# Cross attention: order of panel and x splits, banks given back one by one, and the last head's scaling and splits moved

## The reference, cut to what matters

```
h = h + y @ w_out                                  # y: the two attentions' output
h = h + cross_attention(rms_norm(h, g_cross), rms_norm(mem, g_mem), w_xq, w_xkv, w_xo)

q  = x @ w_xq;  k, v = split(memn @ w_xkv)         # 4 heads of 256
s  = q @ k.T / sqrt(256)                           # per head, 1024 x 256
o  = softmax(s) @ v
return o.reshape(1024, 1024) @ w_xo
```

## Time and profile before

| | us |
|---|---|
| median of 3 runs | 2339.19 |
| lowest and highest | 2332.63, 2339.25 |
| profiled execution, its own time | 2333.39 |
| its span | 2331.6 |
| TensorE busy | 2231.5 |
| VectorE busy | 1375.6 |
| ScalarE busy | 950.6 |
| GpSimd busy | 701.7 |

### The profile page before, as it was taken

One profiled execution on the slowest core, in us unless ns is written; L12 is line 12 of the kernel. 1 busy time (PEld: TensorE's weight loads), 2 busy tenths in 40 slices (PEclk: granted clock), 3 DMA queues, 4 the chain that ended last, 5 costly groups with the idle time before them and its releaser, 6 DMA issues.

```text
span 2331.6 us, 36430 instructions
## 1 busy us (share of the span) xinstructions
PE 2231.5 (96%) x14780; PEld 1758.6 (75%) x14780; DVE 1375.6 (59%) x1787; ACT 950.6 (41%) x1680; POOL 701.7 (30%) x436
## 2 busy tenths in 40 slices
PE   7999999998999998999999999999999999999997
PEld 4777766666688887778888888888676677778885
DVE  6767846668576445475664675523508376567654
ACT  4444457777534222253344334223415412264321
POOL 2312211221211222345655464422131133222221
PEclk9999999999999999999999999999999999999999
DMA  3211101113132100111111111112120011100022
GB/s 132 75 52 55 43 21 55 55 46 118 46 115 76 37 28 28 46 38 61 64 36 54 54 51 41 61 46 91 64 83 28 14 42 37 39 19 13 4 109 81
DMA packets 38555, 125.80 MB, mean 54 GB/s; under 512 B 3856, under 2 KB 4368, under 8 KB 37776
## 3 DMA queue, kind: packets, MB, share of 16 engines
q1 hardware_dynamic: 33936, 103.30, 13.1%
q10 hardware_dynamic: 4480, 20.49, 2.3%
HBM read 114.34 MB, written 8.91 MB: 53 GB/s over the span
## 4 chain that ended last, share of the span: by engine, by line
PE 83%; DVE 9%; ACT 5%; issue 2%; DMA 0%; ACTq 0%; DVEq 0%
PE PS L184 22%; PE PS L186 21%; PE PS L185 21%; PE PS L2243 2%; PE PS L744 2%; PE PS L767 1%; PE PS L1192 1%; DVE arena L1013 1%; PE PS L929 1%; PE PS L894 1%; PE PS L911 1%; PE PS L312 1%; PE PS L1853 1%; DVE arena L393 1%; PE PS L1713 1%
## 5 line engine op out<-in xcount | busy, mean ns | idle before, releaser
L184 PE MATMUL PS<-u_r,w_hi 128*128 128x512 f32 x1184 | 479.0, 405 | 18.8 <-DVE h L581 4.4
L233 POOL TENSOR_TENSOR w_hi<-w_raw,const 128x1024 fp32r<-128x1024 f32 x77 | 152.8, 1985 | 1133.2 <-PE PS L184 1079.3
L186 PE MATMUL PS<-u_r,w_lo 128*128 128x512 f32 x1184 | 462.8, 391 | 0.0
L194 POOL TENSOR_TENSOR w_lo<-w_raw,w_hi 128x1024 fp32r<-128x1024 f32 (+1 forms) x143 | 331.6, 2319 | 325.4 <-ACT w_hi L190 310.6
L185 PE MATMUL PS<-arena_r,w_hi 128*128 128x512 f32 (+1 forms) x888 | 331.9, 374 | 0.0
L184 PEld LDWEIGHTS PS<-u_r,w_hi 128*128 128x128 f32 x1184 | 222.9, 188 | 76.1 <-DVE arena_r L194 7.2
L186 PEld LDWEIGHTS PS<-u_r,w_lo 128*128 128x128 f32 x1184 | 222.8, 188 | 47.8
L184 PE MATMUL PS<-h_r,w_hi 128*128 128x512 f32 x512 | 209.4, 409 | 4.3 <-DVE u_r L401 3.9
L186 PE MATMUL PS<-h_r,w_lo 128*128 128x512 f32 x512 | 201.0, 393 | 0.0
L185 PE MATMUL PS<-y_r,w_hi 128*128 128x512 f32 x512 | 199.5, 390 | 0.0
L1508 DVE TENSOR_TENSOR h<-h,PS 128x512 f32<-128x512 f32 x288 | 181.8, 687 | 21.7 <-PE PS L186 17.6
(11 more groups left out here) (431 smaller groups left out, 4292.1 us busy)
## 6 DMA issues: line engine op xcount, KB each, us to landing
w_raw<-in_w SPq DMA_DIRECT2D x174, 512.0 KB, 3.4
arena<-in_w SPq DMA_DIRECT2D x10, 512.0 KB, 5.6
h<-in_xT ACTq DMA_DIRECT2D x1, 4096.0 KB, 14.6
u<-parked_stream ACTq DMA_DIRECT2D x1, 4096.0 KB, 12.8
out<-arena SPq DMA_DIRECT2D x16, 256.0 KB, 2.0
parked_stream<-h ACTq DMA_DIRECT2D x6, 512.0 KB, 2.6
h<-in_xT SPq DMA_DIRECT2D x8, 256.0 KB, 7.3
h<-in_xT ACTq DMA_DIRECT2D x8, 256.0 KB, 9.2
```

Of the source, the lines that this page charges most:

```text
L184: first = pe.matmul(out, a[0], b[0], start=start, stop=False)
L186: return first, pe.matmul(out, a[1], b[0], start=False, stop=stop)
L194: return e.tensor_tensor(out, x, hi_part.bitcast(F), ALU.subtract)
L233: pool.tensor_tensor(out, src, cst("ones")[:, 0:1].broadcast_to([P, D]), ALU.mult).then_inc(S("w_high"), 1)
```

## The change

Six edits in the cross attention and at its edges:

- ScalarE's loop over the panels of keys and values takes the high part of x's piece of the panel before in place of the panel's own. VectorE's low part of the first half's last piece moves behind the first piece of the second half accordingly.
- kv_evac is raised by one after each of the last four additions of the output projection, in place of by four after all.
- In head 3 the probabilities are scaled by ScalarE (Identity with a scale per partition), behind the next step's exponential, in place of by VectorE. The low parts of the last projection's input come one step later on VectorE.
- Head 3's output is not copied to qcT. Its second half goes to banks 0 and 1, and y2_act and y2_dve read the four banks.
- VectorE raises xo_evac after the last low part of the transposed probabilities instead of after the last copy.
- GpSimd splits the second panel of w_xo only after the twelfth low part of the last projection's input.

```
--- before.py
+++ after.py
@@ -1159,14 +1159,22 @@
             k, h = Y2[n]
             if n == 0:
                 piece_done(act, "xq", 15)
-            act.wait_ge(S("x_o_evac"), 4 * (k // 2) + 2 * h + k % 2 + 1)
-            high(act, in_u(k, h * HALF, (h + 1) * HALF), qcT[:, k, h * HALF:(h + 1) * HALF]).then_inc(S("split_high"), 1)
+            if n >= 12:
+                act.wait_ge(S("x_o_mm"), n + 1)
+            else:
+                act.wait_ge(S("x_o_evac"), 4 * (k // 2) + 2 * h + k % 2 + 1)
+            high(act, in_u(k, h * HALF, (h + 1) * HALF), y2_from(n)).then_inc(S("split_high"), 1)
+
+        def y2_from(n):
+            k, h = Y2[n]
+            return bank(LAST_O_BANKS[n - 12]) if n >= 12 else qcT[:, k, h * HALF:(h + 1) * HALF]
 
         def y2_dve(dve, n):
             k, h = Y2[n]
             dve.wait_ge(S("split_high"), split_from("y2") + n + 1)
-            low(dve, in_y(k, h * HALF, (h + 1) * HALF), qcT[:, k, h * HALF:(h + 1) * HALF], in_u(k, h * HALF, (h + 1) * HALF))\
-                .then_inc(S("split_low"), 1)
+            low(dve, in_y(k, h * HALF, (h + 1) * HALF), y2_from(n), in_u(k, h * HALF, (h + 1) * HALF)).then_inc(S("split_low"), 1)
+
+        LAST_O_BANKS = (4, 5, 0, 1)
 
         def y2_ready(pe, h):
             return lambda k: pe.wait_ge(*split_ready("y2", max(Y2.index((j, h)) for j in range(k + 1)) + 1))
@@ -1210,15 +1218,23 @@
                     h = s // 4
                     pe.wait_ge(S("x_tlow"), 4 * i + 2 * h + 2)
                     pe.wait_ge(*split_ready("xv", 2 * i + 2))
-                    if 2 * i + h >= 1:
+                    if (i, h) == (3, 1):
+                        pe.wait_ge(S("x_exp"), 32)
+                    elif 2 * i + h >= 1:
                         pe.wait_ge(S("x_o_evac"), 4 * i + 2 * h)
                     for dc in range(2):
                         for kt in range(2):
                             c = i * MEM + dc * P
                             half = slice(h * HALF, (h + 1) * HALF)
-                            f, m = product(pe, bank(4 + dc), (v_high(i, kt)[:, dc * P:(dc + 1) * P], Vc_low[:, kt, c:c + P]),
+                            f, m = product(pe, bank(LAST_O_BANKS[2 * h + dc] if i == 3 else 4 + dc), (v_high(i, kt)[:, dc * P:(dc + 1) * P], Vc_low[:, kt, c:c + P]),
                                            (pT[:, kt, half], pT_low[:, kt, half]), kt == 0, kt == 1)
                         m.then_inc(S("x_o_mm"), 1)
+
+        def probs(e, i, t, scaled):
+
+            e.wait_ge(S("x_recip"), 4 * i + t + 1)
+            for q in range(2):
+                scaled(Px[:, t % 2, q, :], er[:, 2 * t + q:2 * t + q + 1]).then_inc(S("x_probs"), 1)
 
         def x_act(act, i):
             def turned(t):
@@ -1238,6 +1254,8 @@
                                        bias=nm[:, 2 * s + q:2 * s + q + 1], accum_out=el[:, 2 * s + q:2 * s + q + 1])\
                            .then_inc(S("x_exp"), 1)
                 if i == 3:
+                    if s >= 1:
+                        probs(act, i, s - 1, lambda out, by: act.activation(out, out, ACT.Identity, scale=by))
                     for n in y2_fill(i, s):
                         y2_act(act, n)
                 if s >= 1:
@@ -1276,21 +1294,21 @@
                     t = s - 1
                     dve.wait_ge(S("x_exp"), 8 * i + 2 * t + 2)
                     dve.reciprocal(er[:, 2 * t:2 * t + 2], el[:, 2 * t:2 * t + 2]).then_inc(S("x_recip"), 1)
-                    dve.wait_ge(S("x_recip"), 4 * i + t + 1)
-                    for q in range(2):
-                        dve.tensor_scalar(Px[:, t % 2, q, :], Px[:, t % 2, q, :], er[:, 2 * t + q:2 * t + q + 1], None,
-                                          ALU.mult).then_inc(S("x_probs"), 1)
-                if s < 4:
-                    for n in y2_fill(i, s):
-                        y2_dve(dve, n)
+                    if i < 3:
+                        probs(dve, i, t, lambda out, by: dve.tensor_scalar(out, out, by, None, ALU.mult))
+                    else:
+                        for n in y2_fill(i, t):
+                            y2_dve(dve, n)
                 if s == 4:
                     turned_low(2)
-                    take_o(0)
+                    if i < 3:
+                        take_o(0)
                 if s == 5:
                     turned_low(3)
                     for n in y2_fill(i, 4):
                         y2_dve(dve, n)
-                    take_o(1)
+                    if i < 3:
+                        take_o(1)
 
 
         ar = Arena()
@@ -2944,21 +2962,22 @@
             split_dve(dve, "mem", 0, in_(mT), mem_split_high, mem_split_low, (in_(mraw), lambda k: vcol("g_mem", k), m_rs, "mem"))
             for q in range(8, 16):
                 add_wo(q)
+                if q >= 12:
+                    dve.wait_ge(S("wo_evac"), q + 5)
+                    dve.sem_inc(S("kv_evac"), 1)
                 if q == 13:
                     kv_low(dve, 0)
-            dve.wait_ge(S("wo_evac"), 20)
-            dve.sem_inc(S("kv_evac"), 4)
             norm_add(dve, "x", *NATURAL[15])
             kv_low(dve, 1)
             for n in range(17):
                 if n < 15:
                     kv_low(dve, n + 2)
                 for h, k in x_beside(n):
-                    split_dve(dve, "x", h, in_(yT), in_u, in_y, (in_(hT), lambda k: vcol("g_cross", k), x_rs, "x"),
-                              ks=[k] if k < KC - 1 else [k, KC])
+                    for x, ks in ([(0, [KC])] if (h, k) == (1, 0) else []) + [(h, [k, KC] if (h, k) == (1, KC - 1) else [k])]:
+                        split_dve(dve, "x", x, in_(yT), in_u, in_y, (in_(hT), lambda k: vcol("g_cross", k), x_rs, "x"), ks=ks)
             for i in range(4):
                 x_dve(dve, i)
-            dve.wait_ge(S("x_o_evac"), 16)
+            dve.wait_ge(S("x_tlow"), 16)
             dve.sem_inc(S("xo_evac"), 4)
             for n in range(12, 16):
                 y2_dve(dve, n)
@@ -3083,9 +3102,15 @@
                 for x in range(2):
                     split_later_panel(pool, i + 1, x, gone=0)
             split_later_panel(pool, 12, 1)
-            with loop(pool, 7) as i:
+            with loop(pool, 3) as i:
                 for x in range(2):
                     split_later_panel(pool, i + 13, x)
+            split_later_panel(pool, 16, 0)
+            pool.wait_ge(*split_ready("y2", 12))
+            split_later_panel(pool, 16, 1)
+            with loop(pool, 3) as i:
+                for x in range(2):
+                    split_later_panel(pool, i + 17, x)
             with loop(pool, ST_GROUPS) as g:
                 st_pool(pool, g)
             with loop(pool, 9) as i:
@@ -3182,9 +3207,9 @@
                     if n == 4:
                         act.wait_ge(*norm_ready("x", 1))
                         act.sem_inc(S("xq_evac"), len(XQ_BANKS))
-                for h, k in x_beside(n):
+                for h, k in x_beside(n - 1):
                     x_split(h, [k])
-            for h, k in x_beside(16):
+            for h, k in x_beside(15) + x_beside(16):
                 x_split(h, [k])
             act.wait_ge(S("v_turned"), V_MEM)
             xq_act(act, 0)
```

9 lines of the change are left out of this document (6 added, 3 removed).

## The result

| | before | changed |
|---|---|---|
| median, us | 2338.43 (5 runs, 2332.63 to 2339.25) | 2322.64 (5 runs, 2320.94 to 2324.12) |
| profiled execution, us | 2333.39 | 2321.39 |
| its span | 2331.6 | 2319.6 |
| the stretch, us | 225.45 | 210.42 |

The ratio is 0.9938, 95% interval 0.9926 to 0.995: 15.8 us faster by the medians, 14.9 forecast; the median of 2322.64 stands beside a forecast of 2321.5 and a range of 2314 to 2328. "The stretch" is used from here on: from the start of the output projection's last matmul to the start of the first matmul of the last projection's third piece (682.44 to 907.89 before). All six edits lie inside it, and it is 15.03 shorter.

A forecast was written before the change was run, and what follows sets the result against it. TensorE was taken as working 96% of the span, so gains could come only from its waits or clock; 1.04 (banks) + 7.75 (x's high parts) + 6.1 (last head) = 14.9 off 2336.3 gave 2321.5 us, range 2314 to 2328.

The forecast's parts named there:

- banks singly: Output projection's end: with banks given back one by one, keys and values start earlier, gain 1.04 us.
- x's high parts later: Keys and values: ScalarE splits x's piece a panel later, so periods fall from 3.54 to 2.88 us; gain 7.75.
- wait at the first transposes: Last head, first step: TensorE's 5.52 us wait for the probabilities falls to 1.5, gain 4.0.
- low clock: Last head: with the long wait gone, TensorE's clock stays up and the slow 6.03 us cycle gives back 1.47.
- dearer steps: Last head: exponential and scaling in one ScalarE queue make two cycles 5.08 us instead of 4.56, 1.04 lost.
- end of the last head: Without the output copies, the idle time before the first panel's last two chunks goes: 1.0 to 1.7 us, 1.7 taken.
- period with the root: Keys and values: one period also holds the root of x's second half; 0.15 us taken off the gain.
- C: Rival: panel loop gets no shorter because x's piece still holds VectorE; only 7.1 us gained, 2329; chance 0.08.
- The moved panel costs nothing: Last head: GpSimd's held-back panel meets VectorE low parts reading PSUM, unstretched; a general slowdown would cost VectorE 4.6 us.
- A: Rival: last head gives half, scaling dearer and the clock still falling once; 10.3 us gained, 2326; chance 0.13.
- B: Rival: raw panels come late, seven loads each 0.5 us late; 11.4 us gained, 2325; chance 0.06.
- D: Rival: short waits in the last head keep TensorE at 1.2 GHz; slower, 2341 us; chance 0.04.

The follow-up runs named there:

- delayed kernel: Changed kernel plus four idle 128x768 copies on ScalarE ahead of the last head's first scaling: stretch 216.13 us, time 2324.90 us (one run).

## Why the prediction was right, step by step

| step | forecast | measured in the profiles |
|---|---|---|
| banks singly | 1.04 | 1.04 (1.27 between two starts, now 0.23) |
| x's high parts later | 7.75 | 7.66 (fourteen periods: 688.69 to 736.91, now 692.44 to 733.00) |
| wait at the first transposes | 4.0 | 4.05 (5.52, now 1.47) |
| low clock | 1.47 | gone; with it the steps are 0.31 shorter in sum, forecast 0.43 |
| dearer steps | 5.08 each | 5.14 each, before 4.56 |
| end of the last head | 1.7 | 1.98 (894.74 to 907.89, now 886.55 to 897.72) |
| sum | 14.9 | 15.03 |

The start of those fourteen periods in the kernel before, on ScalarE:

```profile
688.69 1.06 ACT L190 ACTIVATE w_hi<-arena 128x1024 fp32r<-128x1024 f32 x1 [3.52 <-PE PS L184]
```

**Right for its reasons.** The loop over ScalarE and VectorE was tried alone on the kernel before and stood (7.5). Two more reasons were tried by undoing them in the changed kernel: the copies (1.95 when put back, together with the later xo_evac) and the queue of exponential and scaling (2.66 less without it). The banks gave their 1.04 at their place, though alone they bring only 0.30 of the stretch. Scaling by ScalarE costs 0.91 for two, forecast 0.92. The period with the root lost 0.35, later regained in part by a period of 2.78, so 0.15 was close. The end of the last head gave 1.98, above the prediction's upper bound of 1.7. One slip is in the chances: C is said to be split between faster and same, but 0.88 and 0.08 leave it whole with same.

**Right in sum, loose in credit.** The prediction named three things that free the first transposes: maximum ahead of the low parts, the panel held back, scaling on ScalarE. Two can each be left out: without the hold the stretch is 0.14 longer, and with VectorE scaling the first wait is not even 1.47 but none. The order gives the last 2 us: with the hold alone the wait is 1.98, with hold and order (VectorE scaling) it is gone. Whether the order would do without both others was not run, and the rows speak against it. Without the hold GpSimd's passes lie from 868.46 to 873.12, and VectorE would scale from about 869.0, inside them. The kernel before shows what that does, in its third head, beside the pass from 856.28:

```profile
857.30 3.49 DVE L1281 TENSOR_SCALAR pos_i<-pos_i,er 128x256 f32<-128x256 f32 x2
```

An estimate from these rows: the scalings would end near 873.1, and TensorE, out of work at 870.20, would wait about 3. So the order needs one of the two beside it.

"The moved panel costs nothing" was right, but it also brings next to nothing here; alone on the kernel before it brings 2.65. It costs nothing because of what stands beside it on VectorE. In these traces GpSimd's passes stretch low parts with both inputs in SBUF (three take 5.43 and 5.41, against 1.87 to 1.90) and scalings from SBUF to SBUF (two take 2.85, 3.49 and 4.43, against 0.62), and leave low parts that read PSUM at 0.68 to 0.69. So the rule as the prediction puts it, that with one SBUF input at most VectorE is not shut out, is too wide: it fits the low parts here and not the scalings. With VectorE still scaling, the held-back panel brings a wait of 2.95.

**The rivals.** A (scaling dearer, clock falls) did not come: no granted clock under 1.00 from 640 to 960. B did not: no wait for a raw panel. C fell with the periods of 2.88. D would need a fall in the last head; waits of 1.47, 0.71 and 0.71 did not bring one, a wait of 4.97 did, and even then the clock was back within the next step.

**What the profile alone would have shown wrongly.** It is only 12.0 shorter. 687.30 against 682.44 shows 4.86 lost ahead of the stretch, in unchanged code, and 1.8 came back behind it. From 610 to 625 the kernel before has a clock of 1.00 (the first line), the changed one 0.66 (the second):

```profile
610.00:625.00 15.00, 11.69 (x90) 9.08 (x90) 6.57 (x9) 3.31 (x6) 0.00 (x0) 1.00 0.00 1
```
```profile
610.00:625.00 15.00, 12.24 (x62) 8.64 (x60) 7.60 (x10) 3.79 (x7) 0.00 (x0) 0.66 0.05 18
```

## What to carry to other kernels

Find the loop through the engines that sets a period, and cut it by taking one engine's work an iteration later; compare the longest single engine per period with the period wanted. When work moves from one engine's queue to another's, ask what it now stands behind: here the move cost 0.6 per step until the scaling was put ahead of the exponential. Read a small edit by a stretch between two fixed instructions, since the whole time moves by more than the edit.

## What was not expected of the hardware

The spread of up to 10 us between runs of one kernel goes with TensorE's clock. In the comparison with most runs, 27 of the kernel before took 2330.55 at a mean granted clock of 0.993 up to 2340.41 at 0.987, and the correlation of time and clock is -0.98. Over 13 profiles the span outside the stretch lies between 2103.8 and 2110.0 us; the time at 1.2 GHz outside it (twice one minus the granted clock, summed over windows of 10 us up to 2310) lies between about 24 and 44 us. The correlation is 0.90, the slope 0.27 us per us. The low spells stand in about a dozen fixed places, among them near 320, 610, 980, 1650 and 1840 us, and which of them occur differs from profile to profile of nearly the same program. What decides it in one run is left open, and whether the clock is all of the spread is not shown.

The price of one fall is not fixed either: the step after the wait took 1.47 longer in the kernel before, 1.57 with x's high parts later, 2.33 with banks singly (6.89 against 4.56) and 2.15 in the delayed kernel, after waits of 5.52, 5.52, 5.52 and 4.97. What goes with it is the length of the spell: by windows of half a microsecond the granted clock was at 0.50 for 3.4 us in the first two and for 6.8 us in the last two. What makes a spell short or long is not shown.
